# Memory-attention scores as three matmuls on split queries and keys, in a one-core transformer layer

## The reference, cut to what matters

```
q = rms_norm((h @ w_q).reshape(bsz, t, X_HEADS, X_HEAD_DIM), qn)     # 512 tokens, 4 heads of 128
k = rms_norm(kv[..., :D_X].reshape(bsz, m, X_HEADS, X_HEAD_DIM), kn) # 256 memory rows
s = jnp.einsum('bqhd,bmhd->bhqm', q, k) * (X_HEAD_DIM ** -0.5)
prob = jax.nn.softmax(s, axis=-1)
o = jnp.einsum('bhqm,bmhd->bqhd', prob, v) ; return o @ w_o
```

## Time and profile before

| what | value |
|---|---|
| time, median of 3 runs | 671.92 us (671.22 to 672.23) |
| profiled execution, its time | 671.54 us |
| profiled execution, its span | 669.6 us |
| PE busy | 657.5 us, 98% of the span |
| PE's share of the chain that ended last | 94% |
| DVE, ACT, POOL busy | 488.1, 344.0, 179.2 us |
| granted TensorE clock | 0.999 of full speed |

### The profile page before, as it was taken

The page is one execution under the profiler, slowest core; times in us unless marked ns, Lnnn a source line. Parts: engine busy times, 40 slices in busy tenths (PEclk is TensorE's granted clock), DMA queues, the critical chain, the costliest instruction groups (busy, mean ns, idle before and its releaser), DMA issues.

```text
span 669.6 us, 10584 instructions
## 1 busy us (share of the span) xinstructions
PE 657.5 (98%) x3920; PEld 542.1 (81%) x3920; DVE 488.1 (73%) x799; ACT 344.0 (51%) x593; POOL 179.2 (27%) x183
## 2 busy tenths in 40 slices
PE   7999899999999999999999999999999999999997
PEld 6876788877788788887998888888888888888886
DVE  6999989578756665557697665666656687867967
ACT  6638564867745464664354333333334444554662
POOL 6899996023220102330100111011110121100000
PEclk9999999999999999999999999999999999999999
DMA  8765955666110405030346555555566446654663
GB/s 315 293 206 106 184 127 158 173 187 226 64 64 1 158 0 189 1 126 0 127 180 247 198 184 196 189 199 177 188 216 222 143 174 226 210 190 140 182 196 126
DMA packets 67991, 108.64 MB, mean 162 GB/s; under 512 B 15876, under 2 KB 40621, under 8 KB 66413
## 3 DMA queue, kind: packets, MB, share of 16 engines
q1 hardware_dynamic: 64636, 101.77, 46.4%
q10 hardware_dynamic: 3312, 6.32, 3.1%
HBM read 91.16 MB, written 17.31 MB: 162 GB/s over the span
## 4 chain that ended last, share of the span: by engine, by line
PE 94%; DMA 2%; SPq 1%; ACT 1%; DVE 1%; issue 1%; ACTq 0%; POOL 0%; POOLq 0%; DVEq 0%
PE pb L505 26%; PE pb L507 26%; PE pb L506 26%; PE pb L1959 8%; PE pb L1962 5%; PE pb L2012 4%; DMA F<-scr_u 1%; SPq L662 1%; DMA first<-in_first 1%; ACT F L1001 1%; SPq L651 1%; DVE wring L498 0%; DVE F L1392 0%; ACT wring L1001 0%; ACT wring L487 0%
## 5 line engine op out<-in xcount | busy, mean ns | idle before, releaser
L505 PE MATMUL pb<-xs,wring 128*128 128x512 f32 (+1 forms) x400 | 149.6, 374 | 0.0
L507 PE MATMUL pb<-xs,wring 128*128 128x512 f32 (+1 forms) x400 | 148.9, 372 | 0.0
L506 PE MATMUL pb<-xs,wring 128*128 128x512 f32 (+1 forms) x400 | 148.8, 372 | 0.0
L1398 DVE SCALAR_TENSOR_TENSOR F<-pb,cols,F 128x511 f32<-128x511 f32 x88 | 65.9, 748 | 71.8 <-ACT F L1001 70.3
L505 PE MATMUL pb<-wring,xs 128*128 128x512 f32 x240 | 98.8, 412 | 1.6 <-ACT pbuf L1001 1.4
L1001 ACT ACTIVATE F<-pb,cols 128x512 f32<-128x512 f32 x50 | 38.2, 766 | 115.4 <-PE pb L507 115.4
L495 DVE TENSOR_TENSOR wring<-raw,wring 128x1024 fp32r<-128x1024 f32 x70 | 92.0, 1317 | 6.2 <-ACT wring L484 6.1
L507 PE MATMUL pb<-wring,xs 128*128 128x512 f32 x240 | 93.9, 391 | 0.0
L506 PE MATMUL pb<-wring,xs 128*128 128x512 f32 x240 | 93.7, 390 | 0.0
L505 PEld LDWEIGHTS pb<-xs,wring 128*128 128x128 f32 x400 | 75.3, 188 | 13.5 <-issue 0.6
L507 PEld LDWEIGHTS pb<-xs,wring 128*128 128x128 f32 x400 | 75.3, 188 | 13.2
(11 more groups left out here) (154 smaller groups left out, 1011.0 us busy)
## 6 DMA issues: line engine op xcount, KB each, us to landing
raw<-in_ffn_w_up SPq DMA_DIRECT2D x22, 1024.0 KB, 5.3
F<-in_ffn_w_down SPq DMA_DIRECT2D x11, 1024.0 KB, 5.0
scr_w<-F SPq DMA_DIRECT2D x11, 1024.0 KB, 3.9
F<-in_x SPq DMA_DIRECT2D x8, 512.0 KB, 7.4
raw<-in_w_in ACTq DMA_DIRECT2D x4, 1024.0 KB, 6.4
raw<-in_w_out SPq DMA_DIRECT2D x4, 1024.0 KB, 4.8
raw<-scr_w SPq DMA_DIRECT2D x8, 512.0 KB, 3.9
raw<-scr_w SPq DMA_DIRECT2D x15, 256.0 KB, 4.5
```

Of the source, the lines that this page charges most:

```text
L505: nc.tensor.matmul(ps, lh, rh, start=first, stop=False)
L506: nc.tensor.matmul(ps, lh, rl_, start=False, stop=False)
L507: return nc.tensor.matmul(ps, ll, rh, start=False, stop=last)
L1398: return V.scalar_tensor_tensor(out=o, in0=a, scalar=s1, in1=b, op0=o1, op1=o2)
```

## The change

The queries and keys of the memory attention are kept in two parts, and each score is made by `mm3`.

- Keys: ACT writes the high part of all keys into a new tensor `kx_hi_rows`, in one operation after its last work on the blocked attention. POOL subtracts it from `kxT` in two operations, one for each half of the memory rows, behind its `pow_event` of "ya", and writes the low part into a free part of `bs`.
- Queries: `qx_split(t)` takes the place of `transposed`. DVE reads the same PSUM bank twice, once for the high part and, when that is written, once for the low part. Both go into `xs`, into places whose tile has been used. The product of gain and scale is computed once, by one small ACT operation (`gx`).
- Scores: three f32r matmuls of 256 columns each take the place of one float32 matmul of 256 columns. PE waits for the low keys (`kx_lo`) instead of the evacuation of the keys.

```diff
+        gx = sb("gx", [128, 1])
+        kx_hi_rows = sb("kx_hi_rows", [128, XH, M], f32r)
+        kx_part = [kx_hi_rows.rearrange("p h (m n) -> p h m n", m=MT),
+                   bs.rearrange("p m (h n) -> p h m n", h=XH)[:, :, :, 384:512]]
+        qx_part = [xs[:, part, 0:4, :] for part in range(2)]
...
             for i in range(EVN["ya"], len(EV)):
                 pow_event(i)
+                if EV[i][0] == "ya":
+                    pool.wait_ge(kx_hi, 1)
+                    for m in range(MT):
+                        ins = sub(kx_part[1][:, :, m, :], kxT[:, :, m * 128:(m + 1) * 128],
+                                  kx_part[0][:, :, m, :].bitcast(f32))
+                    ins.then_inc(kx_lo, 1)
...
+            c = COL["x_qn"]
+            A_(gx[:, :], gcol[:, c:c + 1], ACT.Copy, scale=XD ** -0.5).then_inc(gx_ready, 1)
...
             ya_square(TT - 1)
+            after_drain(act, "kx1")
+            A_(kx_hi_rows.rearrange("p h m -> p (h m)"), kxT.rearrange("p h m -> p (h m)"), ACT.Copy).then_inc(kx_hi, 1)
...
+            def qx_split(t):
+                p = read(dve, f"qxt{t}")[:, :].rearrange("p (a b) -> p a b", a=4)
+                hi, lo = (v[:, :, t * 128:(t + 1) * 128] for v in qx_part)
+                if t == 0:
+                    dve.wait_ge(gx_ready, 1)
+                link(V.tensor_scalar_mul(hi, p, gx[:, 0:1]))
+                drained(stt(lo, p, gx[:, 0:1], hi.bitcast(f32), ALU.mult, ALU.subtract), f"qxt{t}")
+
             qx_event(0)
-            transposed("qxt", qT, "x_qn", XD ** -0.5, [0])
+            qx_split(0)
...
-                    transposed("qxt", qT, "x_qn", XD ** -0.5, [1 + s // 4])
+                    qx_split(1 + s // 4)
...
-                filled(mm(p[:, 0:M], qT[:, h, t * 128:(t + 1) * 128], kxT[:, h, :]), f"xs{s}")
+                at = slice(t * 128, (t + 1) * 128)
+                filled(mm3(p[:, 0:M].rearrange("p (m n) -> p m n", m=MT), qx_part[0][:, h, at], qx_part[1][:, h, at],
+                           kx_part[0][:, h, :, :], kx_part[1][:, h, :, :], True, True), f"xs{s}")
...
-            after_drain(pe, "kx0")
-            after_drain(pe, "kx1")
+            pe.wait_ge(kx_lo, 1)
```

More of the change, by code:

```diff
@@ L230, in layer @@
         half_ok, far_zero = sem("half_ok"), sem("far_zero")
-        gq_ready = sem("gq_ready")
+        gq_ready, gx_ready = sem("gq_ready"), sem("gx_ready")
+        kx_hi, kx_lo = sem("kx_hi"), sem("kx_lo")
         relb_ok = sem("relb_ok")
```

## The result

The changed kernel took 672.93 us (median of 20 runs, 671.66 to 674.51), the kernel before 672.10 us in 20 runs beside it. The ratio is 1.0014, with a 95% interval of 1.0007 to 1.0020: a loss of about 0.9 us, inside the bound of 0.2% within which the prediction had put it.

The account below looks back on a forecast made before the run. PE, busy 98%, bounds the kernel, through its own work and its waits for operands. Terms -1.09 + 0.94 + 0.51 + 0.40 = +0.76 us, on the median 671.92, gave 672.7, range 671.0 to 674.0.

Parts of the forecast that it names:

- the forecast's case: Whole kernel: the scores' gain outweighed by three PE waits, +0.76 us, 672.7, own range 672.2 to 673.2; chance 45%.
- The three waits: PE waits at the first residual transposes (+0.94 us), the first score (+0.51) and behind the first exponential (+0.40).
- the fourth term, the scores: Score loop on PE: three f32r passes at 0.120 each gain 0.068 a score, -1.09 us for 16.
- Rival 3: Scores: three passes run at the rate of the columns, 0.320 a score; sum +0.15, 672.1 us; chance 12%.
- rival 5: Scores: weight loads stand bare between short passes; sum +4.0, 676 us; chance 3%.
- The meeting at "ya": DVE's first two root products wait for POOL's key subtractions, making the first residual transposes late; PE loses 0.94 us.
- rival 4: POOL's key subtractions take longer than 1.288 us because of four-piece access; at 1.790 the sum is +1.76, 673.7; chance 15%.
- rival 2: At "ya" DVE and POOL do not meet, or DVE passes between the subtractions; sum -0.18, 671.7 us; chance 17%.
- The first score and the first exponential: Loop start: second query operation delays the first score, +0.51 us; ACT's later first exponential delays PE's transposes, +0.40.
- The later tiles: Query splits after tile 0: hidden, no loss; without cover, each of three tiles would cost up to 0.78 us.
- a wait that I have not seen: Anywhere on PE: the prediction as a whole would be wrong if PE took up the lost time there; no size given.
- Rival 1: Whole kernel: DVE and POOL do not meet and PE finds operands ready; -1.09, 670.8 us; chance 8%.

Follow-up runs that it names:

- The changed order on DVE: Changed kernel with DVE's first query root ahead of its split and the second tile's sum of squares behind step 1's row maximum; ratio 1.0008.
- the half split: Changed kernel with tile 0's query split in two halves of two heads, plus later POOL subtractions and the new DVE order; 672.00 us, ratio 0.9982.
- the four edits: Changed kernel with later POOL subtractions, new DVE order, tile 0's split in two halves, and output weights split a step earlier; 670.94 us, ratio 0.9974.

## Why the prediction was right

**The time and the forecast's case held.** 672.93 lies in the likeliest case's own range of 672.2 to 673.2. The three waits happened where and as they were forecast, and their terms were within 0.04 of the stretch; the fourth term, the scores, was low by 0.23.

**The scores.** The step was the distance of 0.120 between f32r matmuls, and the passes run at that: 0.120 again. The gain is 0.085 in a step of the loop and not 0.068; in the first three, the group that I read it from, it is 0.073. Why a score by itself gains more is open. The 109 ns that the prediction estimated by the Trainium skill, page "TensorE: Matmul & The Clock Gate", section "Back-to-back issue gap", did not stand as firmly against 0.120 as it seemed: that section gives the formula for an isolated matmul, and says that in a stream of weight loads and matmuls both set the spacing. The scores are such a stream, and the trace has 120 ns, at a granted clock of 1.00. Rival 3, the column rate, is out, and so is rival 5, bare weight loads.

**The meeting at "ya".** The order was right to the operation: power, then the two subtractions, with root's first two products behind them, 1.24 and 1.21. The subtractions took 1.286 each against the 1.288 taken from the earlier trace rows, although they read and write in four pieces of 128; so rival 4 is out. Moved behind the root, the same work costs 0.90 less: the meeting is shown as the cause, and rival 2 is out as well. The Trainium skill, page "SBUF — State Buffer", section "Who interferes with whom", has a DVE instruction with two inputs in SBUF, when it is issued second, wait for the whole of a GpSimd instruction that reads SBUF. The trace agrees: the two products end at 233.30 and 234.54, and POOL's subtractions at 233.28 and 234.52.

**The first score and the first exponential.** 0.52 and 0.43 against 0.51 and 0.40. The changed order on DVE takes the second away and leaves the first, and the half split takes most of the first. The 0.11 for a weight load that was not made ahead was too much for transposes: it shows at the score (264.67 to 264.90, 0.23 instead of 0.12), while the two groups of transposes show 0.03 and 0.06.

**The later tiles.** Nothing was predicted for their query splits, and nothing is seen: PE's rows between the first probability transposes and the third unit show no wait.

**What the prediction did not have** is the third unit of the output weights, +0.38, and 0.12 behind it. The last paragraph named "a wait that I have not seen" as what would make the prediction wrong as a whole, if PE took up the lost time there. This one took up nothing; it added to the loss. It could have been read: in the kernel before, PE already lost 0.21 there, so the low part was already late. Every delay of the loop's start then reached ACT and POOL in full, and what PE gained on the way only made it arrive early. The earlier split of that unit shows it (0.64 back). The 0.12 is put down to DVE's addition by the rows alone; it was not tried by itself. This miss of 0.50 was half covered by the scores' 0.23. That the sum came so near, +0.76 against +1.03 in the stretch and +0.83 in the medians, is in part luck.

**Rival 1, the whole gain kept,** is near to what the four edits make: -1.21 in the stretch, 0.21 of it not from the scores. The gain was there, and the change gave it back at five places: the first residual transposes, the first score, the first exponential, the third unit of the output weights and the tile behind it. The edits moved the first four out of the way, up to a small rest at the split; the fifth remains. Their time, 0.26% below or 1.75 us (0.15% to 0.38%, 1.0 to 2.6 us), holds those 1.21.

## What to carry to other kernels

Where one engine is busy 98%, cheaper work on it is worth only what the engines that feed it can follow: look for every operand that is ready with less to spare than the gain, and for those that are late already, before counting the gain. A small DVE product that reads two operands in SBUF should not stand beside a large POOL operation when a waiting engine needs it; the same POOL operations beside two DVE operations that read one operand in PSUM cost nothing. Where a measured time can't tell a microsecond, the length of a stretch behind a common place in PE's list can.

## What was not expected of the hardware

- POOL's subtraction of 128x512 held two DVE products of 128x4 (1.24 and 1.21 instead of 0.16), but not DVE operations of 128x512 with one operand in PSUM: two of these took 0.75 each beside it, their usual time.
- POOL's four pieces of 128 cost it nothing: 1.286, against 1.288 in the earlier trace rows.
- Behind float32 matmuls the first f32r matmul is recorded 0.20 ahead of the next (270.65 and 270.85) and not 0.12. Only distances that enclose both kinds are a price, such as that of a whole step.
